# A mask added on POOL and a bias added by ScalarE in place of two VectorE operations, in the recurrence of a hybrid decoder layer

## Chip, cores and metric

The kernel runs on one core of a Trainium2 chip. The metric is the device time of one execution in microseconds (us), as the median of several runs. The profile shows one execution.

## What is computed

One decoder layer over 1024 prompt tokens and 8 sample tokens, with width 1024. A norm with modulation and the input projection come first, then three groups in parallel (RG-LRU, mLSTM, multi-scale pool), an output projection, and an MLP with squared ReLU. The change lies in the mLSTM group, four heads of width 96, which is worked in eight chunks of 128 tokens, one after the other:

```python
bcum = jnp.cumsum(lfb, axis=-1)
D = bcum[..., :, None] - bcum[..., None, :] + ib[..., None, :]
D = jnp.where(mask, D, -jnp.inf)
g = bcum + m[..., None]
m_t = jnp.maximum(g, jnp.max(D, axis=-1))
inter = jnp.exp(g - m_t)
S = jnp.einsum('bhtd,bhsd->bhts', qb, kb) * jnp.exp(D - m_t[..., None])
num = jnp.einsum('bhts,bhsd->bhtd', S, vb) + inter[..., None] * jnp.einsum('bhvk,bhtk->bhtv', C, qb)
...
C_new = decay[..., None, None] * C + jnp.einsum('bhs,bhsv,bhsk->bhvk', w, vb, kb)
```

The exponent `D - m_t` of a pair (t, s) is the sum of a term of t alone (the negated running maximum, once bcum is taken out of it), a term of s alone (ib - bcum), and the mask.

## The kernel before

Every engine has its own stream of instructions, written out by hand, with semaphores between them. `MIX_ORDER` is a table of steps that all engines walk through in the same order, each issuing what it has to do in a step; so a step's place in the table is its place in every queue. `D:u:c` is a dense product of the input projection, unit u (128 output features) and third c of the tokens (344 columns), three float32r matmuls per block because each factor is split into a high and a low part. The high parts are copies on ScalarE (`W_hi`, `Y_hi`), the low parts are differences on POOL (`W_lo`, `Y_lo`); steps `W:u`, `D:14:c` and later, `YD:c` and `POOLY` carry such splits. `ADA`, `ADT` and `ADM` work on the modulation, and `R:n` are loads of weights that ScalarE's queue issues. Between the dense products stand the small steps of the recurrence, with c now the chunk from 0 to 7:

- `LD:c`: SP loads keys, queries, values and `NM`, the negated running maxima of the chunk's tokens (128 columns of t for four heads, the same on all 128 partitions). `NM` has one buffer. The load of chunk c waits until `NM` has been read for chunk c - 1 (L884).
- `EX:c`: the exponent. On VectorE, `EX` = `NM` + the column of s, broadcast along t (L1885), then the minimum of that and the mask (L1886), both 128x512; then ScalarE takes the exponential in place (L1368). For c > 0 VectorE first waits for the product of chunk c - 1 that read `EX` (bank A).
- `S:c`: TensorE transposes the keys (L2498) and multiplies keys and queries (L2502). `SX:c`: VectorE weights the keys (L1892) and multiplies scores and exponential (L1895).
- `AB:c`: TensorE multiplies queries and state (L2514) and, once L1895 is done, scores and values (L2520). `NU`, `HN`, `HM` on VectorE build the normalised output (L1900 to L1919), with a square root on ScalarE between them (L1371); `U` and `CN` bring the state forward (L2528, L1923, L1925).
- `Y:c`, `YD:c`: the chunk's output is transposed (L2536), gated (L1936) and split.

ScalarE runs copies, exponential, square root, sigmoid and gelu (L1331). Some of these need another table of functions: then an ACT_TABLE_LOAD stands before the operation, at the same line. `SMB`, `SMC` are the sample tokens' branch on VectorE, `POOLV` to `POOLY` the pool group, whose matmuls (L2549) take the banks that `NU` frees.

```python
c = s[1]
if c == 0:
    tell(V.memset(CN[:], 0.0), cn_ready, 1)
    dve.wait_ge(ld_dec, 16)
    dve.wait_ge(ld_mask, 16)
else:
    wait_full(dve, ("A", c - 1))
dve.wait_ge(ld_nm, 16 * (c + 1))
link(V.tensor_tensor(EX[:], NM[:], wide(colh(0, c), LC), ALU.add))
tell(V.tensor_tensor(EX[:], EX[:], over(MASK[:], HEADS), ALU.min), ex_ready, c + 1)
```

Of the kernel before, what the change touches and what calls it, by code (L numbers as in the profile page):

```python
# [87 lines left out]
def unit_of(kind, t):  # L88
# [57 lines left out]
D:9:0  # L146
D:9:1 R:46 R:45 LD:1 ADM:16 EX:0 ADA:17:0 S:0 SX:0 ADA:17:1 W:11 AB:0 R:47
D:9:2 ADT:17 U:0 NU:0 HN:0 CN:0 ADM:17 HM:0 EX:1 ADA:18:0 SMK S:1 SX:1 SMB:0
D:10:0 LD:2
D:10:1 LD:3 AB:1 NU:1 ADA:18:1 U:1 CN:1 HN:1  # L150
D:10:2 HM:1 R:49 R:48 LD:4 EX:2 W:12
D:11:0 SMB:1 S:2 SX:2 AB:2 NU:2 ADT:18 U:2 CN:2 ADM:18 HN:2 R:50
D:11:1 SMB:2 HM:2 R:52 EX:3 ADA:19:0 S:3 SX:3
D:11:2 SMB:3 AB:3 ADA:19:1 W:13 LDO:0 R:51 NU:3
D:12:0 ADT:19 U:3 HN:3 HM:3 R:53 CN:3 ADM:19 LD:5 ADA:20:0 EX:4 R:55
D:12:1 S:4 SX:4 ADA:20:1 Y:0 R:54 SMC AB:4 NU:4
D:12:2 R:56 U:4 ADT:20 HN:4 W:14 YD:0 R:58 HM:4 LD:6
# [132 lines left out]
def build(nc, I, O):  # L290
# [24 lines left out]
    with ExitStack() as ctx:  # L315
# [482 lines left out]
        def _(sp):  # L798
# [26 lines left out]
            for s in plan:  # L825
# [41 lines left out]
                elif k == "LD":  # L867
# [210 lines left out]
        def _(pool):  # L1078
# [25 lines left out]
            for s in plan:  # L1104
# [108 lines left out]
        def _(act):  # L1213
# [55 lines left out]
            for s in plan:  # L1269
# [407 lines left out]
        def _(dve):  # L1677
# [78 lines left out]
            for s in plan:  # L1756
# [1129 lines left out]
```

## Time and profile before

| | |
|---|---|
| median of 3 runs | 1175.29 us (1174.09 to 1179.2) |
| the profiled execution's own time | 1175.78 us |
| its span | 1174.0 us |
| its mean granted TensorE clock | 0.982 of full speed |
| busy: PE, VectorE (DVE), ScalarE (ACT), POOL | 1124.6, 792.8, 473.4, 346.9 us |
| the eight chunks of the recurrence | from about 225 to 385 us |

The span is the time between the first and the last instruction of the execution that the profiler took. Busy time of an engine is the sum of its instructions; "idle before" names the time an engine stood still before an instruction and what released it. PE is TensorE, and "granted clock" is the share of 2.4 GHz at which it was allowed to run: 0.50 is 1.2 GHz.

### The profile page before, as it was taken

To read this page: it belongs to the slowest core of one execution; us is meant where nothing else is said; L and a number is where in the kernel's file an instruction comes from. 1 tells how busy PE (TensorE), PEld (TensorE's weight loads), DVE (VectorE), ACT (ScalarE), POOL (GpSimd) and SP (SyncE) were. 2 spreads that over 40 slices of the span, in tenths; PEclk is the share of its full clock that TensorE was granted. 3 is DMA by queue.
4 is the path that set the end of the run, shared out by engine and by line. 5 is a ranking of instruction groups with operands and counts; after the bars stand their busy time and mean duration, and the time that the engine had idled before them with its cause. 6 is when DMAs were issued, how large, how long until landed. Compare 5 with 4: busy or idle time off the path is not lost.

```text
span 1174.0 us, 19681 instructions
## 1 busy us (share of the span) xinstructions
PE 1124.6 (96%) x7237; PEld 1077.3 (92%) x7237; DVE 792.8 (68%) x1319; ACT 473.4 (40%) x780; POOL 346.9 (30%) x275
## 2 busy tenths in 40 slices
PE   4799999999989999999999999999999999999997
PEld 1598888888979999899999999999999999999996
DVE  4561455478775434678578878778778788788546
ACT  5551355655456344642233332332432433433431
POOL 0442011201434357764032022132131231231352
PEclk9699999998989999999999999999999999999998
DMA  8912523566523722111111111202102202111104
GB/s 302 326 57 88 142 90 126 177 180 218 176 87 113 269 90 73 54 55 37 37 36 55 54 37 55 71 18 71 56 16 75 68 18 72 53 50 58 37 1 145
DMA packets 67846, 109.85 MB, mean 94 GB/s; under 512 B 6435, under 2 KB 42567, under 8 KB 67399
## 3 DMA queue, kind: packets, MB, share of 16 engines
q1 hardware_dynamic: 57574, 84.88, 22.0%
q10 hardware_dynamic: 10208, 24.12, 6.6%
q8 instruction: 41, 0.67, 0.2%
q14 instruction: 23, 0.18, 0.0%
HBM read 96.81 MB, written 12.18 MB: 93 GB/s over the span
## 4 chain that ended last, share of the span: by engine, by line
PE 82%; DVE 9%; ACT 3%; DMA 2%; issue 1%; POOL 1%; SPq 1%; ACTq 0%; POOLq 0%; DVEq 0%
PE D L2407 7%; PE D L2409 7%; PE D L2408 7%; PE D L2591 6%; PE D L2593 5%; PE D L2592 5%; PE X L2593 5%; PE X L2591 5%; PE X L2592 5%; PE X L2663 5%; PE X L2664 5%; PE X L2665 5%; PE D L2663 2%; PE D L2665 2%; PE D L2664 2%; DMA RAWW<-in_WADA 2%
## 5 line engine op out<-in xcount | busy, mean ns | idle before, releaser
L2407 PE MATMUL D<-H_hi,W_hi 128*128 128x344 f32 x472 | 158.6, 336 | 3.7 <-POOL H_lo L1087 3.1
L2409 PE MATMUL D<-H_hi,W_lo 128*128 128x344 f32 x472 | 152.4, 323 | 0.0
L2408 PE MATMUL D<-H_lo,W_hi 128*128 128x344 f32 x472 | 152.4, 323 | 0.0
L1087 POOL TENSOR_TENSOR Y_lo<-FU,Y_hi 128x344 fp32r<-128x344 f32 (+3 forms) x84 | 100.1, 1194 | 154.2 <-ACT Y_hi L1521 88.5
L1082 POOL TENSOR_TENSOR W_lo<-RAWW,W_hi 128x1024 fp32r<-128x1024 f32 x25 | 61.6, 2465 | 182.5 <-ACT W_hi L1234 182.2
L1087 POOL TENSOR_TENSOR Y_lo<-EY,Y_hi 128x344 fp32r<-128x344 f32 (+1 forms) x24 | 38.3, 1598 | 216.3 <-ACT Y_hi L1521 144.5
L2407 PEld LDWEIGHTS D<-H_hi,W_hi 128*128 128x128 f32 x472 | 90.5, 192 | 11.8 <-issue 7.6
L2408 PEld LDWEIGHTS D<-H_lo,W_hi 128*128 128x128 f32 x472 | 90.3, 191 | 0.9 <-issue 0.5
L2409 PEld LDWEIGHTS D<-H_hi,W_lo 128*128 128x128 f32 x472 | 90.2, 191 | 0.0
L2215 DVE SCALAR_TENSOR_TENSOR X<-X,MOD 128x344 f32<-128x344 f32 (+1 forms) x138 | 75.7, 566 | 9.2 <-PE X L2665 9.0
L2663 PE MATMUL X<-Y_hi,W_hi 128*128 128x344 f32 x252 | 80.7, 320 | 0.0
L2664 PE MATMUL X<-Y_lo,W_hi 128*128 128x344 f32 x252 | 80.6, 320 | 0.0
L2665 PE MATMUL X<-Y_hi,W_lo 128*128 128x344 f32 x252 | 80.5, 319 | 0.0
L2017 DVE SCALAR_TENSOR_TENSOR X<-D,MOD,X 128x344 f32<-128x344 f32 (+1 forms) x72 | 41.3, 573 | 45.4 <-PE D L2593 24.7
L2407 PE MATMUL D<-Y_hi,W_hi 128*128 128x344 f32 x192 | 62.0, 323 | 1.5 <-POOL W_lo L1082 1.5
L1099 POOL TENSOR_TENSOR SS<-SS,SQ 128x344 f32<-128x344 f32 x45 | 43.3, 963 | 65.9 <-ACT SQ L1430 40.5
L1087 POOL TENSOR_TENSOR Y_lo<-KEPT,Y_hi 128x344 fp32r<-128x344 f32 x24 | 26.4, 1098 | 120.7 <-ACT Y_hi L1521 120.7
L2408 PE MATMUL D<-Y_lo,W_hi 128*128 128x344 f32 x192 | 61.3, 319 | 0.0
L2409 PE MATMUL D<-Y_hi,W_lo 128*128 128x344 f32 x192 | 61.3, 319 | 0.0
L1556 ACT ACTIVATE W_hi<-RAWW 128x1024 fp32r<-128x1024 f32 x30 | 31.8, 1059 | 64.3 <-PE X L2665 55.6
L2378 PE MATMUL X<-RAWW,CTX 128*32 128x256 f32 x384 | 35.7, 461 | 19.5 <-DMA RAWW<-in_WADA 19.4
L1087 POOL TENSOR_TENSOR H_lo<-FU,H_hi 128x344 fp32r<-128x344 f32 (+2 forms) x33 | 29.9, 914 | 66.2 <-ACT FU L1252 50.7
(416 smaller groups left out, 3455.1 us busy)
## 6 DMA issues: line engine op xcount, KB each, us to landing
RAWW<-in_W SPq DMA_DIRECT2D x76, 512.0 KB, 3.6
RAWW<-in_WADA ACTq DMA_DIRECT2D x28, 512.0 KB, 4.1
RAWW<-in_WADA SPq DMA_DIRECT2D x20, 512.0 KB, 8.0
RAWW<-in_W ACTq DMA_DIRECT2D x18, 512.0 KB, 3.7
X0T<-in_x SPq DMA_DIRECT2D x3, 1376.0 KB, 12.8
out_y<-OUTN SPq DMA_DIRECT2D x24, 172.0 KB
X<-in_x SPq DMA_DIRECT2D x8, 344.0 KB, 5.3
NM<-nm_d SPq DMA_DIRECT2D x8, 256.0 KB, 5.3
```

What stands on the lines that cost most here:

```text
L1082: nc.gpsimd.tensor_tensor(lo_v, RAWW[:, raw, :] if src is None else src[:], hi_v.bitcast(F32), ALU.subtract).then_inc(w_lo_ready, 1)
L1087: nc.gpsimd.tensor_tensor(lo_v, fu_v, hi_v.bitcast(F32), ALU.subtract).then_inc(lo_ready, 1)
L2215: V.scalar_tensor_tensor(out=X[:, m, c * CH:c * CH + w], in0=ps[:, 0:w], scalar=MOD[:, 5 * KT + m, 0:1], in1=X[:, m, c * CH:c * CH + w], o ...
L2407: T.matmul(out, w_h, hi[:, kt, a:b], start=(kt == 0), stop=False)
L2408: T.matmul(out, w_h, lo[:, kt, a:b], start=False, stop=False)
L2409: one = T.matmul(out, w_l, hi[:, kt, a:b], start=False, stop=(kt == KT - 1))
L2591: T.matmul(out, w_h, hi(kt), start=(kt == 0 and not onto), stop=False, skip_group_check=onto)
L2592: T.matmul(out, w_h, lo(kt), start=False, stop=False, skip_group_check=onto)
L2593: one = T.matmul(out, w_l, hi(kt), start=False, stop=(kt == n - 1), skip_group_check=onto)
L2663: T.matmul(bank[:, 0:CH], w_hi[:, a:a + P], h, start=(start and k == 0), stop=False, skip_group_check=onto)
L2664: T.matmul(bank[:, 0:CH], w_hi[:, a:a + P], l, start=False, stop=False, skip_group_check=onto)
L2665: one = T.matmul(bank[:, 0:CH], w_lo[:, a:a + P], h, start=False, stop=(stop and k == 1), skip_group_check=onto)
```

## The change

POOL gets a step of its own, `NX:c`, which adds the mask to `NM` in place once its load has landed. ScalarE's `EX:c` reads `NM` and writes `EX`, one head at a time, with the column of s as the bias of the exponential. The two VectorE operations are gone, and the waits that stood before them are now ScalarE's (for bank A of chunk c - 1, and for POOL's add). SP's load of the next `NM` waits for the exponential in place of the VectorE operation. The mask is 0 or -3e38, so that adding it and taking the minimum give the same exponential.

```diff
-D:9:1 R:46 R:45 LD:1 ADM:16 EX:0 ADA:17:0 S:0 SX:0 ADA:17:1 W:11 AB:0 R:47
-D:9:2 ADT:17 U:0 NU:0 HN:0 CN:0 ADM:17 HM:0 EX:1 ADA:18:0 SMK S:1 SX:1 SMB:0
+D:9:1 R:46 R:45 LD:1 ADM:16 NX:0 EX:0 ADA:17:0 S:0 SX:0 ADA:17:1 W:11 AB:0 R:47
+D:9:2 ADT:17 U:0 NU:0 NX:1 HN:0 CN:0 ADM:17 HM:0 EX:1 ADA:18:0 SMK S:1 SX:1 SMB:0
...
-D:14:0 Y:2 ADM:21 EX:6 YD:2
+D:14:0 Y:2 ADM:21 NX:6 EX:6 YD:2
...
-D:15:0 U:6 Y:4 POOL:1:0 R:62 CN:6 POOLY:1:0 ADA:23:0 EX:7 POOL:1:1 W:16 R:64 YD:4
+D:15:0 U:6 Y:4 POOL:1:0 R:62 CN:6 POOLY:1:0 ADA:23:0 NX:7 EX:7 POOL:1:1 W:16 R:64 YD:4
...
                     if c >= 1:
-                        sp.wait_ge(ex_ready, c)
+                        sp.wait_ge(ex_exp, c)
...
+                elif k == "NX":
+                    if s[1] == 0:
+                        pool.wait_ge(ld_mask, 16)
+                    pool.wait_ge(ld_nm, 16 * (s[1] + 1))
+                    nc.gpsimd.tensor_tensor(NM[:], NM[:], over(MASK[:], HEADS), ALU.add).then_inc(nm_masked, 1)
...
                 elif k == "EX":
-                    act.wait_ge(ex_ready, s[1] + 1)
-                    nc.scalar.activation(EX[:], EX[:], ACT.Exp).then_inc(ex_exp, 1)
+                    c = s[1]
+                    if c == 0:
+                        b, n = use[("G4",)]
+                        act.wait_ge(x_free[b], n + 1)
+                    else:
+                        wait_full(act, ("A", c - 1))
+                    act.wait_ge(nm_masked, c + 1)
+                    for h in range(HEADS):
+                        one = nc.scalar.activation(EX[:, h, :], NM[:, h, :], ACT.Exp, bias=colh(0, c)[:, h:h + 1])
+                    one.then_inc(ex_exp, 1)
...
                 elif k == "EX":
-                    c = s[1]
-                    if c == 0:
+                    if s[1] == 0:
                         tell(V.memset(CN[:], 0.0), cn_ready, 1)
                         dve.wait_ge(ld_dec, 16)
-                        dve.wait_ge(ld_mask, 16)
-                    else:
-                        wait_full(dve, ("A", c - 1))
-                    dve.wait_ge(ld_nm, 16 * (c + 1))
-                    link(V.tensor_tensor(EX[:], NM[:], wide(colh(0, c), LC), ALU.add))
-                    tell(V.tensor_tensor(EX[:], EX[:], over(MASK[:], HEADS), ALU.min), ex_ready, c + 1)
```

`NX:2` to `NX:5` stand likewise ahead of their `EX`, further away from it: behind `NU:1`, `NU:2`, `NU:3` and `NU:4`.

POOL's queue through the stretch of the recurrence, before and after as one piece of the difference. L1082 splits weights, L1128 is the new add.

```order
-L1082 TENSOR_TENSOR W_lo<-RAWW,W_hi 128x1024 x12
+L1082 TENSOR_TENSOR W_lo<-RAWW,W_hi 128x1024 x8
+L1128 TENSOR_TENSOR NM<-NM,MASK 128x512
+L1082 TENSOR_TENSOR W_lo<-RAWW,W_hi 128x1024
+L1128 TENSOR_TENSOR NM<-NM,MASK 128x512 x2
+L1082 TENSOR_TENSOR W_lo<-RAWW,W_hi 128x1024
+L1128 TENSOR_TENSOR NM<-NM,MASK 128x512
+L1082 TENSOR_TENSOR W_lo<-RAWW,W_hi 128x1024
+L1128 TENSOR_TENSOR NM<-NM,MASK 128x512 x2
+L1082 TENSOR_TENSOR W_lo<-RAWW,W_hi 128x1024
 L1087 TENSOR_TENSOR Y_lo<-FU,Y_hi 128x3x128 x2
```

The adds of chunks 0 to 5 stand between the weight splits of the units 10 to 14. Further down the same queue, the adds of chunks 6 and 7 stand between the splits of the gated outputs (L1087).

```order
 L1087 TENSOR_TENSOR Y_lo<-FU,Y_hi 128x344
+L1128 TENSOR_TENSOR NM<-NM,MASK 128x512
 L1087 TENSOR_TENSOR Y_lo<-FU,Y_hi 128x3x128
 L1087 TENSOR_TENSOR Y_lo<-FU,Y_hi 128x344 x2
 L1087 TENSOR_TENSOR Y_lo<-FU,Y_hi 128x3x128
 L1087 TENSOR_TENSOR Y_lo<-FU,Y_hi 128x344 x5
+L1128 TENSOR_TENSOR NM<-NM,MASK 128x512
 L1082 TENSOR_TENSOR W_lo<-RAWW,W_hi 128x1024
```

The first of them now follows the split of `D:14:0`, the second the two splits of `D:15:0` and `POOLY:1:0`.

ScalarE's queue around `EX:6`, with what each instruction waits for, before:

```order
L1331 ACTIVATE GT<-D 128x344 [waits dense0_full]
L1239 ACTIVATE Y_hi<-FU 128x344 [waits full_ready]
L1368 ACT_TABLE_LOAD
L1368 ACTIVATE EX<-EX 128x512 [waits ex_ready]
L1239 ACTIVATE Y_hi<-FU 128x3x128 [waits full_ready]
L1331 ACT_TABLE_LOAD [waits full_ready]
L1331 ACTIVATE GT<-D 128x344 [waits dense1_full]
```

and after:

```order
L1336 ACTIVATE GT<-D 128x344 [waits dense0_full]
L1244 ACTIVATE Y_hi<-FU 128x344 [waits full_ready]
L1380 ACT_TABLE_LOAD [waits nm_masked]
L1380 ACTIVATE EX<-NM,COL 128x128 [waits X1_full]
L1380 ACTIVATE EX<-NM,COL 128x128 x3
L1244 ACTIVATE Y_hi<-FU 128x3x128 [waits full_ready]
L1336 ACT_TABLE_LOAD [waits full_ready]
L1336 ACTIVATE GT<-D 128x344 [waits dense1_full]
```

The one exponential has become four, and the wait for the add (`nm_masked`) stands at the table load, where the load had no wait before; this holds for all eight chunks.

## Rows read from the trace of the kernel before

**Rows 1.** The page, busy time and share of the span of the matmul engine.

```profile
...
PE 1124.6 (96%) x7237; PEld 1077.3 (92%) x7237; DVE 792.8 (68%) x1319; ACT 473.4 (40%) x780; POOL 346.9 (30%) x275
...
```

**Rows 2.** Waits of PE, 225 to 385 us: engine line <- released by: us, times, longest.

```profile
...
PE X L2549 <- DVE NUM L1903: 3.7, 1, 3.7
PE X L2520 <- DVE EX L1895: 2.9, 3, 1.7
PE D L2407 <- POOL W_lo L1082: 1.5, 1, 1.5
...
```

**Rows 3.** Windows: us, busy (x) of PE, PEld, DVE, ACT, POOL; PEclk, DMA share, GB/s.

```profile
...
232.00:240.00 8.00, 7.00 (x60) 5.85 (x60) 5.12 (x12) 2.64 (x4) 0.00 (x0) 1.00 0.91 274
...
268.00:275.00 7.00, 7.00 (x34) 7.00 (x35) 4.69 (x13) 1.39 (x2) 0.65 (x1) 0.54 0.52 174
...
382.00:392.00 10.00, 8.48 (x54) 8.36 (x54) 4.86 (x5) 3.44 (x6) 5.48 (x5) 1.00 0.64 211
...
```

**Rows 4.** The page, DMA issues: x count, KB each, us to landing.

```profile
...
NM<-nm_d SPq DMA_DIRECT2D x8, 256.0 KB, 5.3
```

**Rows 5.** Groups by line and form, ScalarE: xcount | busy us, mean ns | idle before.

```profile
...
L1368 ACT ACTIVATE EX<-EX 128x512 f32<-128x512 f32 x8 | 5.1, 632 | 5.8 <-DVE EX L1886 5.7
...
```

**Rows 6.** The same view for POOL.

```profile
...
L1060 POOL TENSOR_TENSOR PA<-ST 128x1023 f32<-128x1023 f32 x1 | 1.9, 1890 | 0.0
...
L1209 POOL TENSOR_TENSOR OUTN<-XG,INVS 128x344 f32<-128x344 f32 x2 | 1.8, 908 | 6.2 <-ACT INVS L1673 6.2
...
```

**Rows 7.** One line of the program, L1362: duration ns min/median/max, first and last start.

```profile
...
L1362 ACT ACTIVATE GR<-GR,MPC x1: 405/405/405, 134.4 to 134.4; 36x128 f32<-36x128 f32 x1
...
```

**Rows 8.** Timelines at chunk 0: start us, us, engine line op xcount [idle before <- releaser].

```profile
...
233.29 0.69 DVE L1885 TENSOR_TENSOR EX<-NM,COL 128x512 f32<-128x512 f32 x1 [1.25 <-DMA NM<-nm_d]
...
233.96 1.28 ACT L1368 ACT_TABLE_LOAD   x1 [1.35 <-issue]
...
235.97 0.69 DVE L1895 TENSOR_TENSOR EX<-X,EX 128x512 f32<-128x512 f32 x1 [0.67 <-ACT EX L1368]
...
236.72 1.13 PE L2520 MATMUL X<-VB,EX 128*128 128x97 f32 x8 [1.00 <-DVE EX L1895]
...
```

**Rows 9.** Timelines at chunk 2.

```profile
...
264.65 0.63 ACT L1368 ACTIVATE EX<-EX 128x512 f32<-128x512 f32 x1
...
267.08 0.69 DVE L1895 TENSOR_TENSOR EX<-X,EX 128x512 f32<-128x512 f32 x1
...
267.82 1.41 PE L2520 MATMUL X<-VB,EX 128*128 128x97 f32 x8 [1.67 <-DVE EX L1895]
...
```

**Rows 10.** Timelines of POOL and DVE where both read SBUF, 286 us.

```profile
...
286.67 2.40 POOL L1082 TENSOR_TENSOR W_lo<-RAWW,W_hi 128x1024 fp32r<-128x1024 f32 x1 [18.02 <-ACT W_hi L1234]
...
286.86 2.62 DVE L1912 TENSOR_TENSOR HM<-NUM,SM 128x384 f32<-128x384 f32 x1
...
```

**Rows 11.** Timelines at chunk 6.

```profile
...
327.99 1.12 POOL L1087 TENSOR_TENSOR Y_lo<-FU,Y_hi 128x344 fp32r<-128x344 f32 x1 [2.28 <-ACT Y_hi L1239]
...
330.85 0.52 ACT L1239 ACTIVATE Y_hi<-FU 128x384 fp32r<-128x384 f32 x1 [0.53 <-DVE FU L1936]
...
332.69 0.46 ACT L1331 ACTIVATE GT<-D 128x344 f32<-128x344 f32 x1
...
334.32 0.69 DVE L1895 TENSOR_TENSOR EX<-X,EX 128x512 f32<-128x512 f32 x1
...
335.07 1.13 PE L2520 MATMUL X<-VB,EX 128*128 128x97 f32 x8 [0.19 <-DVE EX L1895]
...
```

**Rows 12.** Timelines at chunk 7.

```profile
...
355.41 2.27 POOL L1087 TENSOR_TENSOR Y_lo<-FU,Y_hi 128x344 fp32r<-128x344 f32 x2 [3.34 <-ACT Y_hi L1239]
...
358.27 0.64 ACT L1368 ACTIVATE EX<-EX 128x512 f32<-128x512 f32 x1 [0.51 <-DVE EX L1886]
...
358.81 1.04 ACT L1234 ACTIVATE W_hi<-RAWW 128x1024 fp32r<-128x1024 f32 x1
...
366.82 0.46 ACT L1331 ACTIVATE GT<-D 128x344 f32<-128x344 f32 x1 [1.05 <-PE D L2409]
...
```

More of the change, by code:

```diff
@@ L146 @@
 D:9:0
-D:9:1 R:46 R:45 LD:1 ADM:16 EX:0 ADA:17:0 S:0 SX:0 ADA:17:1 W:11 AB:0 R:47
-D:9:2 ADT:17 U:0 NU:0 HN:0 CN:0 ADM:17 HM:0 EX:1 ADA:18:0 SMK S:1 SX:1 SMB:0
+D:9:1 R:46 R:45 LD:1 ADM:16 NX:0 EX:0 ADA:17:0 S:0 SX:0 ADA:17:1 W:11 AB:0 R:47
+D:9:2 ADT:17 U:0 NU:0 NX:1 HN:0 CN:0 ADM:17 HM:0 EX:1 ADA:18:0 SMK S:1 SX:1 SMB:0
 D:10:0 LD:2
-D:10:1 LD:3 AB:1 NU:1 ADA:18:1 U:1 CN:1 HN:1
+D:10:1 LD:3 AB:1 NU:1 NX:2 ADA:18:1 U:1 CN:1 HN:1
 D:10:2 HM:1 R:49 R:48 LD:4 EX:2 W:12
-D:11:0 SMB:1 S:2 SX:2 AB:2 NU:2 ADT:18 U:2 CN:2 ADM:18 HN:2 R:50
+D:11:0 SMB:1 S:2 SX:2 AB:2 NU:2 NX:3 ADT:18 U:2 CN:2 ADM:18 HN:2 R:50
 D:11:1 SMB:2 HM:2 R:52 EX:3 ADA:19:0 S:3 SX:3
-D:11:2 SMB:3 AB:3 ADA:19:1 W:13 LDO:0 R:51 NU:3
+D:11:2 SMB:3 AB:3 ADA:19:1 W:13 LDO:0 R:51 NU:3 NX:4
 D:12:0 ADT:19 U:3 HN:3 HM:3 R:53 CN:3 ADM:19 LD:5 ADA:20:0 EX:4 R:55
-D:12:1 S:4 SX:4 ADA:20:1 Y:0 R:54 SMC AB:4 NU:4
+D:12:1 S:4 SX:4 ADA:20:1 Y:0 R:54 SMC AB:4 NU:4 NX:5
 D:12:2 R:56 U:4 ADT:20 HN:4 W:14 YD:0 R:58 HM:4 LD:6
@@ L512, in build @@
         ld_nm, ld_o, ld_mask = sem("ld_nm"), sem("ld_o"), sem("ld_mask")
-        ex_ready, ex_exp, cn_ready = sem("ex_ready"), sem("ex_exp"), sem("cn_ready")
+        nm_masked, ex_exp, cn_ready = sem("nm_masked"), sem("ex_exp"), sem("cn_ready")
         z_ready, z_root, hm_ready = sem("z_ready"), sem("z_root"), sem("hm_ready")
```

## The prediction, made before the changed kernel was run

> **What bounds the kernel now.** I read the page first: TensorE is busy 96% of the span, VectorE 68%, ScalarE 40%, POOL 30% [rows 1]. So work taken off VectorE is worth only what TensorE waits for VectorE, and that is the second view. All eight chunks of the recurrence run between 225 and 385 us, and nothing outside that stretch is touched. There TensorE's waits are few: 3.7 us in one piece before the pool group's matmuls, 2.9 us in three pieces for the exponent times scores (L1895), 1.5 us for a weight split (L2407) [rows 2]. The last two numbers matter most: only the 2.9 us sit directly behind the operations that the change moves. Third, the granted clock by stretch. From 232 to 240 us, a wait of 1.00 us included, it was 1.00; from 268 to 275 us, right behind a wait of 1.67 us, it was 0.54, nearly all of it at 1.2 GHz; from 382 to 392 us, a wait of 1.5 us included, it was 1.00 again [rows 3, 8, 9]. The stretch at 0.54 lost 7.0 x 0.46 = 3.2 us of work, more than the wait ahead of it. So a wait just above those that were harmless costs its own length and may cost 3.2 us more; whether it does is not in my hands.
>
> **What is removed.** VectorE loses 16 operations of 0.69 us [rows 8], 11 us in all. Where its queue is what TensorE waits for, this is a gain of up to 1.4 us per chunk. It is that only at chunk 2, below. At chunks 1, 3, 4 and 5 TensorE does not wait for the product of scores and exponent: the cover is the dense products of the next unit, matmuls that need nothing of the recurrence. If that cover were gone, each would be worth its 1.4 us.
>
> **What is added, with prices.** (a) POOL adds 128x512, never seen here. Two-input float operations on POOL took 0.908 us for 344 columns and 1.890 us for 1023 [rows 6]; between them a column costs 1.45 ns, so 512 come to 1.15 us. These two rows are also the bounds, 0.9 and 1.9; I take 1.15, since 512 lies between them and near the first. (b) ScalarE runs four exponentials of 128 columns with a column as bias where it ran one of 512 in 0.632 us [rows 5]. The one exponential of 128 columns with a bias column took 0.405 us [rows 7], and a following ScalarE operation starts 0.10 us before its forerunner ends (358.27 + 0.64 against 358.81) [rows 12]. Four cost 3 x 0.305 + 0.405 = 1.32 us. Bounds: 0.63 if the column is free, 1.62 with no overlap. (c) The wait for POOL now hangs on the load of the exponential's table, as the order of ScalarE shows; before, the load had no wait and ran while VectorE still worked (233.96 to 235.24, while the second VectorE operation ended at 233.29 + 2 x 0.69 = 234.7) [rows 8]. So its 1.28 us follow POOL's add where they lay beside VectorE's. (d) The next load of the row maxima waits for the exponential, 1 to 4 us later than for VectorE's add. It lands 5.3 us after issue [rows 4], and the starts of two chunks' products lie 13 us apart or more; I cost that at nothing from chunk 1 on, and the stores and loads of o behind it on SP's queue likewise. If a load came late after all, POOL's add would wait for it and ScalarE with it.
>
> POOL's queue is in order, so an add that waits for its load holds what is behind it: splits of weights, which TensorE needs only a unit later. The other direction costs: chunks 6 and 7 have their add placed behind splits which wait for ScalarE.
>
> **The sum, chunk by chunk.**
> Chunk 0. The row maxima land at 233.25, VectorE starts at 233.29 and multiplies at 235.97; TensorE waits 1.00 us for it [rows 8]. Now: POOL 233.3 to 234.45, table to 235.8, exponentials to 237.15, product at 237.25. Later by 1.3 us: +1.3. TensorE's wait becomes 2.3 us.
> Chunk 2. All runs 1.3 us later. VectorE is 1.4 us freer and the exponentials, begun at 264.65 + 1.3, end at 267.27; the product starts at 267.35 where 267.08 + 1.3 = 268.38 would stand [rows 9]. Gain 1.0 us, and the wait of 1.67 us shrinks to 0.7 us. ScalarE, not VectorE, is then late next. -1.0.
> Chunk 6. POOL's add follows the split that ends at 329.11; added and signalled at 330.35, table at 331.65, exponentials at 332.95. The copy of Y_hi behind them began at 330.85 and now begins at 332.85, so the gelu at 332.69, the product at 334.32 and TensorE's matmuls at 335.07 all come 2.0 us later [rows 11]. VectorE's windows of the pool group follow them, and the wait of 3.7 us behind is not a cushion, because VectorE is what it waits for [rows 2]. +2.0.
> Chunk 7. The add follows two splits that end at 357.68: 358.9, table 360.2, exponentials 361.5 instead of 358.91. The gelu at 366.82 had 1.05 us of idle before it, which takes part of the 2.6 us [rows 12]. From there a closed chain runs to the split for L2407 and its 1.5 us [rows 2]. +1.5.
> Together +1.3 - 1.0 + 2.0 + 1.5 = +3.8 us. The clock: a wait of 0.7 us should spare the low stretch at 268, -3.2; of the two waits that grow well past 1.67 us (2.3 at chunk 0, about 3.0 at the end) I expect one to bring a low stretch, +3.2. The profiled execution took 1175.78 us with a span of 1174.0 and stands 0.5 us above the median of 1175.29. So 1175.78 + 3.8 = 1179.6, or **1179.1** as a median: 0.3% slower, inside what a measurement here can tell from no change (0.5%, 5.9 us).
>
> POOL's price, row against page: the rows give 1.15 us, 1.7 times VectorE's 0.69. The Trainium skill, "GPSIMD Engine Reference", section "Engine selection", advises VectorE for elementwise work and puts two-input operations on GpSimd at about twice its time. That would be 1.38 us and add 0.2 us at each of three chunks, 0.7 us in all: 1179.8.
>
> **The rivals.**
> *Both grown waits lower the clock.* 3.8 - 3.2 + 6.4 = +7.0: 1182.3. For it: 2.3 and 3.0 us are both longer than the 1.67 us behind which the clock fell. Against: part of the loss at chunk 0 fits into a later wait. It decides from the point where chunk 0's product starts more than about 0.7 us late. This one ends slower.
> *POOL holds up VectorE.* A VectorE operation on two SBUF tiles took 2.62 us, ending as POOL's split of 2.40 us did, where a wider one takes 0.69 [rows 8, 10]. The eight adds are 9.2 us of such time on POOL. Most meet VectorE idle or reading PSUM. Chunk 5's would land on the samples' chain near 297 us, behind which TensorE already waits, and cost up to 1.2 us, chunk 2's half of that: +3.8 + 1.8 = +5.6, 1180.9, and with one more low stretch 1184.1. The Trainium skill says the same in the same reference, section "Key points": GpSimd shares its SBUF interfaces with VectorE, contending with instructions of two SBUF inputs. The trace agrees by its 2.62 us.
> *No low stretch at all.* +3.8 - 3.2 = +0.6: 1175.9. For it: no wait up to 1.5 us was followed by one. Against: 2.3 and 3.0 us are longer.
> *VectorE was the bound after all.* Then 16 x 0.72 with gaps, 11.5 us, come back: 1163.8. Against: TensorE is at 96%, and its waits for the product are 2.9 us in all [rows 1, 2].
> That the change does not do what it says would show as an unchanged VectorE; the order shows its two operations gone, so I give it nothing.
>
> **How the numbers follow.** Forecast 0.50, its own bounds 1176 to 1182 (prices of POOL and bias at their ends); both waits lower the clock 0.22; POOL holds up VectorE 0.15; no low stretch 0.10; VectorE the bound 0.03. Slower by over 5.9 us (above 1181.2): all of the first rival, 0.12 of the second, 0.03 of the forecast's upper end, 0.37. Faster by as much: 0.03. Between: 0.60. The range from 1175.5 to 1185.0 leaves out a tenth at either end.
>
> **What would show it.** Right: VectorE busy 11 us less, ScalarE 5 us more, POOL 9 us more; the table load at L1380 starting after POOL's add at chunks 0, 6 and 7; the product of chunk 0 at 237.2; the wait at 268 below 1 us and the clock at 1.00 behind it; the exponentials of chunks 6 and 7 about 2 us later than before, relative to the matmuls beside them. Wrong: the table load starting before the add ends; TensorE's wait at chunk 0 unchanged; or a total wait between 225 and 385 us that falls by more than 2 us.

## The result and the profile after

| | before | after |
|---|---|---|
| median | 1175.68 us (12 runs) | 1180.96 us (12 runs, 1178.87 to 1186.17) |
| profiled execution, its span | 1175.78, 1174.0 us | 1181.11, 1179.3 us |

The ratio is 1.0052, with a 95% interval of 1.0039 to 1.0065, or 6.1 us of 1175. The quotient of the two medians is a little less, 1.0045: they lie 5.3 us apart, as do the profiled executions. The sum had 3.8 us. The interval lies clear of 1, so the sign is certain; the size is known to a microsecond or two.

The page of the kernel after, busy times by engine:

```profile
PE 1126.4 (96%) x7237; PEld 1078.5 (91%) x7237; DVE 782.9 (66%) x1303; ACT 478.5 (41%) x804; POOL 356.7 (30%) x283
```

Against [rows 1], VectorE has 16 instructions and 9.9 us less, ScalarE 24 instructions and 5.1 us more, POOL 8 instructions and 9.8 us more. The forecast had 11 us less, 5 more and 9 more. So the work moved as the change says, and the time rose. What TensorE waited for between 225 and 390 us tells more (line, what released it: us in total, times, longest):

```profile
PE X L2526 <- DVE EX L1901: 6.0, 3, 2.8
PE X L2555 <- DVE NUM L1909: 2.4, 1, 2.4
PE X L2542 <- DVE MOD L1730: 2.0, 1, 2.0
...
PE X L2542 <- DVEq L1947: 1.3, 1, 1.3
...
```

L2526 and L1901 are L2520 and L1895 of before: 2.9 us of waits for the product of scores and exponential [rows 2] became 6.0. The wait before the pool group, L2555, fell from 3.7 to 2.4 us: part of what chunk 6 lost was taken out of it.

To keep effects apart I cut out the stretch in which the change acts: from the first selector matmul of chunk 0 (PE, L2392 before, L2398 after) to the start of the weight split at the end of chunk 7 (POOL, L1082). The windows of before and of after (length; busy PE, PEld, DVE, ACT, POOL; granted clock; DMA share, GB/s):

```profile
223.87:381.13 157.26, 147.40 (x1043) 136.04 (x1044) 116.05 (x234) 82.86 (x121) 45.91 (x36) 0.96 0.53 161
```

```profile
223.67:385.46 161.79, 148.27 (x1043) 136.18 (x1044) 105.53 (x217) 87.90 (x145) 55.87 (x44) 0.96 0.52 158
```

The stretch is 4.5 us longer. TensorE is idle 161.79 - 148.27 = 13.5 us of it, 9.9 before: 3.7 us are waiting, 0.9 us matmuls that take longer. From the end of the stretch to the end of the span it is 792.9 us before and 793.8 after (1174.0 - 381.13 and 1179.3 - 385.46), and 792.4 to 794.1 in the runs below, whose code there is the same, so I make nothing of that 1.0 us. Ahead of the stretch one execution differs from the next by more: the first selector matmul starts anywhere from 221.5 to 224.9 us, in kernels that are the same up to there. That is why times are compared by the ratios of many runs, and mechanisms within the stretch.

The granted clock after, in windows of PE alone (length, busy, clock, DMA share, GB/s), and one of before near the same place of the program as the last:

```profile
238.00:242.00 4.00, 3.67 (x16) 0.57 1.04 283
268.00:275.00 7.00, 5.87 (x47) 1.00 0.86 288
337.00:341.00 4.00, 4.00 (x23) 0.57 0.35 129
347.00:355.00 8.00, 7.90 (x26) 0.57 0.71 196
```

```profile
342.00:351.00 9.00, 6.24 (x18) 4.85 (x19) 8.08 (x16) 6.30 (x11) 4.28 (x4) 0.62 0.43 120
```

The low stretch at 268 us [rows 3] is gone, as forecast. Two new ones of half its size stand at 238 and 337 us (4.00 x 0.43 = 1.7 us lost each). The one behind the pool group's wait was there before too (9.00 x 0.38 = 3.4 us) and still is (8.00 x 0.43 = 3.4). In all, the clock lost 6.8 us before and 6.8 us after.

**Chunk 0 after**, timeline:

```profile
233.58 1.27 POOL L1128 TENSOR_TENSOR NM<-NM,MASK 128x512 f32<-128x512 f32 x1 [7.22 <-DMA NM<-nm_d]
234.92 1.28 ACT L1380 ACT_TABLE_LOAD   x1 [2.52 <-POOL NM L1128]
236.22 1.28 ACT L1380 ACTIVATE EX<-NM,COL 128x128 f32<-128x128 f32 x4
237.58 0.69 DVE L1901 TENSOR_TENSOR EX<-X,EX 128x512 f32<-128x512 f32 x1 [3.93 <-ACT EX L1380]
238.33 2.02 PE L2526 MATMUL X<-VB,EX 128*128 128x97 f32 x8 [2.82 <-DVE EX L1901]
```

Three operations in a row, none beside another: ScalarE stood idle 2.52 us and then loaded a table. In [rows 8] that load ran while VectorE was still at the second of its two operations.

**Chunk 2 after:**

```profile
267.86 1.28 ACT L1380 ACTIVATE EX<-NM,COL 128x128 f32<-128x128 f32 x4
269.23 0.69 DVE L1901 TENSOR_TENSOR EX<-X,EX 128x512 f32<-128x512 f32 x1 [0.48 <-ACT EX L1380]
269.97 1.13 PE L2526 MATMUL X<-VB,EX 128*128 128x97 f32 x8 [1.13 <-DVE EX L1901]
```

The wait is 1.13 us where [rows 9] had 1.67, and VectorE now waits for ScalarE (0.48 us).

**POOL and VectorE between chunks 3 and 4:**

```profile
285.68 2.40 POOL L1082 TENSOR_TENSOR W_lo<-RAWW,W_hi 128x1024 fp32r<-128x1024 f32 x1 [11.58 <-ACT W_hi L1239]
286.52 1.57 DVE L1913 SCALAR_TENSOR_TENSOR SM<-NUM 128x4 f32<-128x4 f32 x1
288.03 1.27 POOL L1128 TENSOR_TENSOR NM<-NM,MASK 128x512 f32<-128x512 f32 x1
288.12 1.20 DVE L1914 TENSOR_TENSOR SM<-SM,COL 128x4 f32<-128x4 f32 x1
```

Two VectorE operations on four columns end with the POOL operation they run beside, one with the split (288.08), the next with the new add (289.30). Before, both took 0.17 us, and one wider operation lost 2.06 us to the split (2.62 us where it takes 0.56 elsewhere) [rows 10]. So POOL holds up VectorE in both kernels.

**Chunk 6 after:**

```profile
328.03 0.92 POOL L1087 TENSOR_TENSOR Y_lo<-FU,Y_hi 128x344 fp32r<-128x344 f32 x1 [2.25 <-ACT Y_hi L1244]
328.91 1.29 POOL L1128 TENSOR_TENSOR NM<-NM,MASK 128x512 f32<-128x512 f32 x1
330.28 1.28 ACT L1380 ACT_TABLE_LOAD   x1 [2.32 <-POOL NM L1128]
331.57 1.28 ACT L1380 ACTIVATE EX<-NM,COL 128x128 f32<-128x128 f32 x4
...
334.58 0.46 ACT L1336 ACTIVATE GT<-D 128x344 f32<-128x344 f32 x1
...
336.96 1.76 PE L2526 MATMUL X<-VB,EX 128*128 128x97 f32 x8 [2.04 <-DVE EX L1901]
```

Split, add, table load, exponentials, each released by the one before. The gelu moved from 332.69 [rows 11] to 334.58 and TensorE's wait from 0.19 to 2.04 us.

**Chunk 7 after:**

```profile
358.13 1.97 POOL L1087 TENSOR_TENSOR Y_lo<-FU,Y_hi 128x344 fp32r<-128x344 f32 x2 [3.92 <-ACT Y_hi L1244]
360.06 1.29 POOL L1128 TENSOR_TENSOR NM<-NM,MASK 128x512 f32<-128x512 f32 x1
361.43 1.28 ACT L1380 ACT_TABLE_LOAD   x1 [2.33 <-POOL NM L1128]
362.72 0.40 ACT L1380 ACTIVATE EX<-NM,COL 128x128 f32<-128x128 f32 x1
...
370.97 0.46 ACT L1336 ACTIVATE GT<-D 128x344 f32<-128x344 f32 x1
```

The same chain. The gelu of [rows 12], 366.82 before, starts at 370.97 and has no idle time left before it.

Where the 4.5 us came from can be read at TensorE's waits, each counted from the first selector matmul (before 223.87, after 223.67). The two marks of before that no row above shows:

```profile
304.19 0.58 PE L2392 MATMUL X<-SEL,ADS 128*128 128x9 f32 x4 [0.90 <-DVEq L1941]
...
344.76 2.63 PE L2549 MATMUL X<-ST,BDP 128*128 128x344 f32 x4 [3.72 <-DVE NUM L1903]
```

and of after:

```profile
303.69 0.58 PE L2398 MATMUL X<-SEL,ADS 128*128 128x9 f32 x4 [0.90 <-DVEq L1947]
...
346.90 2.03 PE L2555 MATMUL X<-ST,BDP 128*128 128x344 f32 x4 [2.44 <-DVE NUM L1909]
```

| mark | before | after | late by | since the mark above | of it idle | of it busy |
|---|---|---|---|---|---|---|
| scores times values, chunk 0 | 12.85 | 14.66 | 1.8 | +1.8 | +1.8 | 0 |
| the same, chunk 2 | 43.95 | 46.30 | 2.35 | +0.5 | -1.0 | +1.55 |
| selector, behind chunk 4 | 80.32 | 80.02 | -0.3 | -2.65 | +0.3 | -2.95 |
| scores times values, chunk 6 | 111.20 | 113.29 | 2.1 | +2.4 | +2.4 | 0 |
| pool group's matmuls | 120.89 | 123.23 | 2.3 | +0.25 | -1.3 | +1.55 |
| weight split, end of chunk 7 | 157.26 | 161.79 | 4.5 | +2.2 | +1.45 | +0.75 |

The last two columns part each piece into the time that TensorE stood still and the time that its matmuls took, from the windows between the marks. The matmuls are the same ones, so the busy column is the clock: a new low stretch behind chunk 0, the one at 268 us gone, a new one at 337 us. The 0.75 us of the last line is the old stretch at the pool group. Before, its first 1.9 us (342.9 to 344.76) lay in TensorE's wait and cost nothing; after, nearly all of it lies behind the wait.

### The profile page after: what moved, and what is told of

The parts are those of the page before. It is cut to its first block, busy times and chain, and to the rows that moved or that the text cites. A ratio compares the mean times of both kernels' runs of the same rounds, so it can differ in the third digit from the quotient of the medians.

```text
span 1179.3 us, 19696 instructions
## 1 busy us (share of the span) xinstructions
PE 1126.4 (96%) x7237; PEld 1078.5 (91%) x7237; DVE 782.9 (66%) x1303; ACT 478.5 (41%) x804; POOL 356.7 (30%) x283
## 4 chain that ended last, share of the span: by engine, by line
PE 79%; DVE 9%; ACT 5%; DMA 2%; POOL 2%; issue 2%; SPq 1%; ACTq 0%; POOLq 0%; DVEq 0%
PE D L2413 6%; PE D L2415 6%; PE D L2414 6%; PE D L2597 5%; PE D L2599 5%; PE D L2598 5%; PE X L2599 5%; PE X L2597 5%; PE X L2598 5%; PE X L2669 5%; PE X L2671 5%; PE X L2670 5%; PE D L2669 2%; PE D L2671 2%; PE D L2670 2%
## 5 line engine op out<-in xcount | busy, mean ns | idle before, releaser
L1087 POOL TENSOR_TENSOR Y_lo<-FU,Y_hi 128x344 fp32r<-128x344 f32 (+3 forms) x84 | 99.5, 1187 | 154.6 <-ACT Y_hi L1534 87.4
L1082 POOL TENSOR_TENSOR W_lo<-RAWW,W_hi 128x1024 fp32r<-128x1024 f32 x25 | 61.7, 2468 | 147.1 <-ACT W_hi L1239 146.8
L1087 POOL TENSOR_TENSOR Y_lo<-EY,Y_hi 128x344 fp32r<-128x344 f32 (+1 forms) x24 | 38.4, 1599 | 216.3 <-ACT Y_hi L1534 144.5
L1087 POOL TENSOR_TENSOR Y_lo<-KEPT,Y_hi 128x344 fp32r<-128x344 f32 x24 | 26.3, 1098 | 121.8 <-ACT Y_hi L1534 121.8
L1087 POOL TENSOR_TENSOR H_lo<-FU,H_hi 128x344 fp32r<-128x344 f32 (+2 forms) x33 | 29.9, 914 | 66.1 <-ACT FU L1257 50.5
## 6 DMA issues: line engine op xcount, KB each, us to landing
X0T<-in_x SPq DMA_DIRECT2D x3, 1376.0 KB, 12.5
```

The lines of the kernel that those rows point to most:

```text
L1082: nc.gpsimd.tensor_tensor(lo_v, RAWW[:, raw, :] if src is None else src[:], hi_v.bitcast(F32), ALU.subtract).then_inc(w_lo_ready, 1)
L1087: nc.gpsimd.tensor_tensor(lo_v, fu_v, hi_v.bitcast(F32), ALU.subtract).then_inc(lo_ready, 1)
```

## The experiments

My theory: the loss is the table load and four exponentials in series behind an add, and POOL's queue where the add stands behind splits. The rivals: POOL's adds as such, by holding up VectorE; and the clock. Each kernel below was timed in five rounds beside the kernel before. Stretch and TensorE's idle time in it are cut as above; the clock column is the time that the granted clock lost in it, (1 - clock) times length.

| kernel | median | ratio to before, interval | stretch | idle | clock |
|---|---|---|---|---|---|
| before | 1175.0 | | 157.3 | 9.9 | 6.8 |
| after | 1181.0 | 1.0052 (1.0039 to 1.0065) | 161.8 | 13.5 | 6.8 |
| waits swapped | 1176.85 | 1.0013 (1.0 to 1.0026) | 156.9 | 10.7 | 5.1 |
| adds of 6, 7 ahead | 1178.17 | 1.0037 (1.0022 to 1.0053) | 157.8 | 11.5 | 5.1 |
| both | 1176.37 | 1.0007 (0.9994 to 1.002) | 157.6 | 11.3 | 5.1 |
| chunk 0 as before | 1177.78 | 1.0031 (1.0015 to 1.0046) | 159.1 | 11.1 | 6.8 |
| only chunk 0 changed | 1179.47 | 1.0037 (1.0025 to 1.0049) | 161.9 | 12.0 | 10.2 |
| no POOL | 1180.31 | 1.0041 (1.0025 to 1.0058) | 163.5 | 12.5 | 10.2 |
| no POOL, swapped | 1175.22 | 1.0003 (0.9986 to 1.0021) | 159.4 | 10.2 | 8.5 |
| no bias | 1177.92 | 1.0032 (1.0017 to 1.0048) | 159.9 | 12.0 | 6.8 |
| no bias, adds ahead | 1175.24 | 1.001 (0.9989 to 1.003) | 155.0 | 10.2 | 3.4 |
| chunks 1 to 5 changed | 1173.85 | 0.9995 (0.9978 to 1.0012) | 155.9 | 9.6 | 5.1 |
| the same, swapped | 1173.64 | 1.0004 (0.9987 to 1.0021) | 155.7 | 10.9 | 3.4 |
| chunk 0 as before, both | 1174.98 | 0.9997 (0.9984 to 1.0011) | 156.9 | 10.3 | 5.1 |

Stretch, idle and clock are of one execution each, the ratios of all runs; where they differ the ratio decides. Two ratios whose intervals overlap are not surely different. The median of before is that of the last runs, 1174.98 to 1175.68 us in the others; each ratio is to the runs of before beside it.

### ScalarE's two waits swapped

```diff
 c = s[1]
+act.wait_ge(nm_masked, c + 1)
 if c == 0:
     b, n = use[("G4",)]
     act.wait_ge(x_free[b], n + 1)
 else:
     wait_full(act, ("A", c - 1))
-act.wait_ge(nm_masked, c + 1)
 for h in range(HEADS):
```

The last wait written goes to the table load, the one before it to the first exponential. Nothing else differs.

> Only ScalarE's two waits before the exponentials change places, so that the table load carries the wait for bank A (long fulfilled) and the first exponential carries the wait for POOL's add. Mine (the table load behind the wait is part of the loss at chunks 0, 6 and 7): the product of chunk 0 starts 1.3 us earlier than in the changed kernel, TensorE's wait there falls from 2.8 to about 1.5 us, gelu of chunks 6 and 7 come 1.3 us earlier each; 3 x 1.3 = 3.8 us, and 3.2 us more if the low stretch of the clock at 238 us goes: 1174 to 1177 us. Rival (POOL's adds hold up VectorE, or the four exponentials cost it): the load's place does nothing, 1181 us.

Measured: 1.0013, 4.6 us less than with the change (0.0039 x 1175), and the two intervals do not meet; of idle time 2.8 us less. TensorE's wait at chunk 0 fell from 2.82 to 1.59 us, with a low stretch behind it as before. The timeline at chunk 0, and at chunk 6:

```profile
232.05 1.27 POOL L1128 TENSOR_TENSOR NM<-NM,MASK 128x512 f32<-128x512 f32 x1 [6.63 <-DMA NM<-nm_d]
232.74 1.28 ACT L1380 ACT_TABLE_LOAD   x1 [1.29 <-DVE KW L1898]
234.04 1.28 ACT L1380 ACTIVATE EX<-NM,COL 128x128 f32<-128x128 f32 x4
...
326.54 1.29 POOL L1128 TENSOR_TENSOR NM<-NM,MASK 128x512 f32<-128x512 f32 x1
...
327.86 1.28 ACT L1380 ACTIVATE EX<-NM,COL 128x128 f32<-128x128 f32 x4 [0.98 <-POOL NM L1128]
```

The load now runs ahead of POOL's add at chunk 6, under the split (it started at 325.60) and half under it at chunk 0, where it waited for the bank. Order alone gives back most of the loss: shown.

### The adds of chunks 6 and 7 ahead of POOL's splits

```diff
-D:13:2 ADT:21 R:59 U:5 CN:5
-D:14:0 Y:2 ADM:21 NX:6 EX:6 YD:2
+D:13:2 ADT:21 R:59 U:5 NX:6 CN:5
+D:14:0 Y:2 ADM:21 EX:6 YD:2
...
-    HM:6
-D:15:0 ... ADA:23:0 NX:7 EX:7 ...
+    NX:7 HM:6
+D:15:0 ... ADA:23:0 EX:7 ...
```

> Only the places of POOL's adds of chunks 6 and 7 in its queue change: each is put ahead of the splits it followed. Mine: the exponentials of chunk 6 end about 2.0 us and those of chunk 7 about 2.6 us earlier, which is worth 2.0 + 1.5 = 3.5 us: 1177.5 us, with chunk 0 as in the changed kernel. Rival (POOL holds up VectorE wherever it works): the adds cost the same at another place, 1181 us. If the row maxima land late, POOL stands still for them and the splits come late: slower than 1181 us.

Measured: 1.0037, 1.8 us less by the ratios, 2.8 by the medians; the intervals overlap, so by the times alone this gain is not shown. The trace shows where it comes from. POOL's add stands at 325.76, the table load at 328.34 waits for nothing, and TensorE has no wait left for chunk 6's product, where it was 2.04 us. In exchange the add meets work of VectorE: it took 1.66 us instead of 1.29, and TensorE's wait for `MOD` right behind it is 2.36 us where it was 2.00.

### Both

> The two waits of ScalarE swapped, and the adds of chunks 6 and 7 placed ahead of the weight splits. My theory: the table load behind the add is the larger loss (the swap alone gave 4.3 us back), and the place of the adds has little left to give once the load runs under them: chunk 6's wait of 0.71 us goes, and about 1 us at chunk 7; the split for the dense product at the end of that stretch (379.59 with the swap alone) comes near 378.3, TensorE's wait for the recurrence's product at chunk 6 is gone, and the median is about 1175.3 us. Rival A, the two gains add up: 1174.1 or less. Rival B, POOL's adds in the earlier place meet VectorE's pairs of SBUF tiles and give it back: 1176.9 or more.

Measured: 1.0007, between my 1175.3 and rival B, and not to be told from the swap alone (0.0006 apart, with intervals of 0.0013 either way). Rival A, that the gains add up (1174.1, a ratio of 0.9992), lies just outside the interval. Both edits take the table load from behind the add at chunks 6 and 7, so they compete for the same microseconds.

### Chunk 0 alone, both ways

The first kernel gives chunk 0 its two VectorE operations and single exponential back (`OLD = (0,)`), the second does so for all others (`OLD = (1, ..., 7)`). In both, SP's load of the next row maxima waits for the exponential.

```diff
+elif k == "EX" and s[1] in OLD:
+    act.wait_ge(ex_ready, n_old(s[1]))
+    nc.scalar.activation(EX[:], EX[:], ACT.Exp).then_inc(ex_exp, 1)
```

> Chunk 0 as before the change (VectorE adds and takes the minimum, one exponential), chunks 1 to 7 as changed. Mine: TensorE's wait at chunk 0 is 1.0 us again and no low stretch follows; the wait at chunk 2 stays under 1 us and the clock at 1.00 there too; the delays at chunks 6 and 7 remain: 1175.7 - 1.0 - 3.2 + 3.5 = 1175.0 us. Rival (the loss is spread over all chunks, by POOL beside VectorE or by ScalarE's 5 us more): a seventh or an eighth of 5.3 us is saved, 1180.3 us.

> Chunk 0 as changed, chunks 1 to 7 as before (but SP's load of the next row maxima still waits for the exponential). Mine: a wait of 2.8 us at chunk 0 with a low stretch behind it, +1.6 + 3.2 us less what later waits take in; whether the wait at chunk 2 (1.67 us) still brings its own low stretch decides between 1180 and 1177 us. Rival (spread loss): an eighth of 5.3 us, 1176.4 us.

Measured: 1.0031 without the change at chunk 0, where I had 1175.0 us and 1177.78 were measured: a miss. With it there alone, 1.0037, as expected. Taken by themselves the parts cost 3.6 and 4.3 us, together more than the 6.1 us of the whole (0.0052 x 1175), though by no more than the intervals allow. The traces show one reason why they need not add up. With chunk 0 alone changed, lateness of 1.6 us reaches chunk 2, whose VectorE is no freer than before, and the wait there grows to 2.15 us; with three full low stretches the clock lost 10.2 us in all. With all chunks changed, chunk 2 gives 1.0 us back and spares its low stretch. With chunk 0 as before, TensorE waited 0.93 us for the product, but two short waits for transfers came together, and the clock was low from 243 to 248 us, a low stretch that I had not expected (a second one, from 325 to 330 us, stood behind the wait of 2.00 us for `MOD`):

```profile
242.43 0.64 PE L2402 MATMUL X<-RAWW,CTX 128*32 128x256 f32 x8 [0.70 <-DMA RAWW<-in_WADA]
...
243.68 0.78 PE L2522 MATMUL X<-IDN,K 96*128 96x96 f32 x4 [0.61 <-DMA VB<-v_d]
```

### POOL left out; and with the waits swapped

VectorE adds the mask to the row maxima in place, ScalarE the column. The second kernel swaps ScalarE's waits as above.

```diff
...
-nc.gpsimd.tensor_tensor(NM[:], NM[:], over(MASK[:], HEADS), ALU.add).then_inc(nm_masked, 1)
...
+tell(V.tensor_tensor(NM[:], NM[:], over(MASK[:], HEADS), ALU.add), nm_masked, s[1] + 1)
```

> POOL is left out: VectorE adds the mask in place (0.69 us), ScalarE adds the column as bias in four exponentials, the table load keeps its place behind the add. My theory (the load behind the add, and the four exponentials, are the price; POOL's share is its 0.6 us longer add and its queue at chunks 6 and 7): chunk 0's load starts at 234.0, the exponentials end at 236.6, its product starts at 236.7 (237.58 with the change, 235.97 before), the exponentials of chunks 6 and 7 need not wait for POOL's splits, VectorE is busy about 788 us, and the median is 1177 to 1178. Rival, contention of POOL with VectorE is what cost most: without POOL it is as fast as before or faster, 1175 or less.

> The kernel in which VectorE adds the mask in place, ScalarE the column, and POOL does nothing, now with ScalarE's two waits swapped, so that the table load no longer waits for VectorE's add. Stretch and idle are taken from the first selector matmul of chunk 0 to the start of the weight split at the end of chunk 7: before 157.3 us with 9.9 us of TensorE idle, with the change 161.8 and 13.5, without POOL and unswapped 163.5 and 12.5. My theory, the table load behind the add is the larger loss: every exponential whose add comes late ends 1.2 us earlier, the wait at chunk 0 falls from 2.2 to about 0.9 us and that at chunk 2 from 1.8 to about 0.6 us, both without a low stretch behind them; the stretch is about 158.5 us and the median 1176. Rival, the four exponentials and VectorE's add in its queue are the cost: it stays above 161 us, and the median at 1179 or more.

Measured: 1.0041 without POOL, 1180.31 us; I had 1177 to 1178. Leaving POOL's adds out saves nothing that the ratios can show (1.0041 against 1.0052, with overlapping intervals) and 1.0 us of idle time, though VectorE takes eight adds back for it. So the adds as such, and their contention, are not the main cost: this rival falls, but for a share of about 1 us. The miss is the clock again. VectorE multiplied for chunk 0 at 235.79, and waits of 2.16 us there and 1.78 us at chunk 2 both brought a full low stretch. Swapped, the ratio is 1.0003, 4.5 us less, the same amount as with POOL, and again the intervals do not meet. The table load without POOL, then swapped:

```profile
232.37 0.69 DVE L1890 TENSOR_TENSOR NM<-NM,MASK 128x512 f32<-128x512 f32 x1 [1.66 <-DMA NM<-nm_d]
233.13 1.28 ACT L1375 ACT_TABLE_LOAD   x1 [1.86 <-DVE NM L1890]
```

```profile
231.41 0.69 DVE L1890 TENSOR_TENSOR NM<-NM,MASK 128x512 f32<-128x512 f32 x1 [1.79 <-DMA NM<-nm_d]
231.47 1.28 ACT L1375 ACT_TABLE_LOAD   x1 [1.28 <-issue]
232.77 1.28 ACT L1375 ACTIVATE EX<-NM,COL 128x128 f32<-128x128 f32 x4
```

The waits I had expected to fall to 0.9 and 0.6 us fell to 1.58 and 1.19. At chunk 0 the chain is then no longer than before: from the first operation on the row maxima to the multiplication it is 2.72 us (231.41 to 234.13), in the kernel before 2.68 (233.29 to 235.97), with the change 4.00. The wait is longer than the 1.00 us of before because the load landed 0.5 us later. So the second VectorE operation that is gone pays for the three more exponentials, once the table load is out of the way.

### The bias left out; and with the adds ahead

POOL adds the mask, VectorE the column into `EX`, ScalarE takes one exponential of 512 columns, its table load without a wait. The second kernel puts the adds of chunks 6 and 7 ahead of the splits.

```diff
...
+dve.wait_ge(nm_masked, s[1] + 1)
+tell(V.tensor_tensor(EX[:], NM[:], wide(colh(0, s[1]), LC), ALU.add), ex_ready, s[1] + 1)
```

> POOL adds the mask (1.28 us), VectorE adds the column (0.69 us), ScalarE takes one exponential of 512 columns, whose table load has no wait ahead of it. My theory: chunk 0's product starts near 236.0 as before and the wait there is about 1.1 us; chunks 6 and 7 still have their add behind POOL's splits, 1.5 to 2 us later than before; median 1176.5 us, within 1.5 us of the kernel before. Rival, POOL's adds themselves (contention on SBUF and its queue) are the cost: 1179 or more, near the change's 1181.

> POOL adds the mask, VectorE the column, ScalarE takes one exponential; the adds of chunks 6 and 7 now ahead of POOL's weight splits. My theory: what this way cost over the kernel before (idle 12.0 us against 9.9 in the stretch) is POOL's queue at chunks 6 and 7; chunk 6's wait of 1.5 us goes, chunk 7's exponential is on time, idle is about 10.5 us, one low stretch fewer, and the median is 1175.5. Rival, VectorE held up by the add that waits for POOL (2.18 us for one of them) is the cost: 1177.5 or more, as with the adds behind the splits.

Measured: 1.0032, then 1.001. Here no table load stands behind POOL, and 3.8 us are lost all the same, more than I had (1176.5 us, 1177.92 measured): the wait at chunk 0 was 2.01 us for an expected 1.1. With the adds ahead 1.2 us are left. At chunk 6 TensorE's wait was 1.52 us with the add behind the split and gone with it ahead. So POOL's queue is a second place where time is lost, beside the table load. Its size is less sure: 2.6 us by the ratios, whose intervals overlap, and the traces differ by 3.4 us of clock, half of it at chunk 0, ahead of anything that this edit moves.

### Chunks 1 to 5 changed; the same with the waits swapped

> Chunks 0, 6 and 7 as before the change, chunks 1 to 5 as changed, nothing swapped. My theory: chunks 1 to 5 are where the change costs nothing and spares the wait of 1.7 us at chunk 2, so TensorE's idle time in the stretch is 9 to 9.5 us (9.9 before), chunk 6 starts no later against the matmuls beside it, and the median is 1174 to 1175.5, as before or a little less. Rival, POOL's adds beside VectorE's pairs (the small operations of 1.57 and 1.20 us near 287 us) cost as much as the freed VectorE gives: idle of 10.5 us or more and a median of 1176.5 or more.

> As the kernel with only chunks 1 to 5 changed, with ScalarE's two waits swapped. My theory: in these chunks POOL adds the mask long before the column is there, so the wait that the table load carries is that for the column, at every one of them; the swap lets the load run before it and each exponential starts 1.2 us earlier, but TensorE waits for none of them except at chunk 2. So 0 to 0.8 us less than without the swap: median 1173.8 to 1175. Rival: the exponentials 1.2 us earlier meet other work of VectorE and move a wait elsewhere, 1175.5 or more.

Measured: 0.9995 and 1.0004, both no different from before. Where the add has room in POOL's queue, the change costs nothing and what it frees is worth nothing that can be measured; the idle time went from 9.9 to 9.6 us in the one and to 10.9 in the other, where 1.0 us of it is a longer wait at the selector behind chunk 4 (1.86 us for 0.90). On the swap my expectation had the waits the wrong way round: here it puts the wait for the bank on the table load. It made no difference, since neither wait held the load in chunks 2 to 5.

### Chunk 0 as before, waits swapped, adds ahead

> Chunk 0 as before the change (two VectorE operations, one exponential), chunks 1 to 7 as changed with the waits swapped and the adds of chunks 6 and 7 ahead of the splits. My theory: chunk 0's wait is 0.9 us and no low stretch stands behind it; what the changed way gives at chunk 2 stays (no wait of 1.67 us and no low stretch at 268 us), so this is the fastest of all, about 1173.5 us, that is 1.7 us faster than the kernel before. Rival: a low stretch comes somewhere else instead, as behind the waits near 243 us when chunk 0 alone went back: then 1176, no better than the kernel before.

Measured: 0.9997. I had expected 1.7 us less than before. The idle time is 10.3 us. The load of chunk 0's row maxima landed 1.2 us later after the first selector matmul than in the trace of before, TensorE waited 1.67 us there, and the clock fell. So no kernel that was run is faster than the one before by more than the measurement's uncertainty.

## Why the prediction was right

The forecast was a loss of 3.8 us from four places, and a clock that gives back as much as it takes. The trace shows all four places with their mechanisms, close to their size, and 4.5 us in the stretch: 3.7 of waiting and 0.9 of slower matmuls.

- **Chunk 0, +1.3.** Measured 1.8 at the mark. POOL's add started 9.91 us after the selector matmul where VectorE's started 9.42 us after it, so 0.5 us is a later landing, and 1.3 us the chain. VectorE multiplied at 237.58; 237.25 had been forecast.
- **Chunk 2, -1.0.** Measured -1.0. VectorE's last reduction of chunk 1 came 3.4 us late, counted from the selector matmul (260.01 before, 263.17 after), the product of chunk 2 only 2.35. The wait is 1.13 us rather than 0.7, and not below the 1 us that I had named as a sign, because the clock had made everything ahead of it late too.
- **Chunk 6, +2.0.** Measured +2.4, of which 0.5 us is the longer wait for `MOD` at 328 us (2.00, before 1.46), and 1.9 us the exponentials. That longer wait stands in every kernel in which chunk 5 has its four exponentials, without POOL's adds too (2.0 to 2.4 us), and is not in the sum.
- **Chunk 7, +1.5.** Measured +1.45 of idle time. The exponentials ended 5.3 us late against the selector matmul (358.91, then 364.00), the gelu 4.35: the 1.05 us of idle time took its part, as forecast. Of the 5.3, 2.9 were there before the splits (the gelu of the dense product ahead, 353.75, then 356.46), so the add and what hangs on it made 2.4 us for a forecast 2.6.
- **Between chunk 2 and the selector behind chunk 4, nothing in the sum.** Measured +0.3 of idle time, a wait of 0.31 us for `MOD` at 294 us; the wait at the selector is 0.90 us in both. That is all that the second rival, POOL beside VectorE, can have cost here; I had up to 1.8 us for it. Without POOL's adds and with the waits swapped the idle time of this piece is as long, 1.2 us.
- **The clock, -3.2 and +3.2.** By the granted clock -3.4 and +1.7 +1.7, equal sums, but not as I argued. Both grown waits lowered the clock, as the first rival says, and each for half of what I priced; that the two halves made up the one stretch forecast was luck. In matmul time it was -2.95, +1.55 and +1.55, and +0.75 for the stretch at the pool group, which no row of mine had: +0.9 for a forecast 0. The stretch at 337 us cost little, because TensorE would otherwise have waited longer for VectorE before the pool group (-1.3 us of idle time). I had written that this wait was no cushion. It is none for ScalarE's lateness and it is one for slow matmuls.
- **Prices.** POOL's add, the tile's view after:

```profile
L1380 ACT ACTIVATE EX<-NM,COL x32: 384/387/403, 236.2 to 363.6; 128x128 f32<-128x128 f32 x32
...
L1128 POOL TENSOR_TENSOR NM<-NM,MASK x8: 1267/1288/1554, 233.6 to 360.1; 128x512 f32<-128x512 f32 x8
```

It took 1.29 us, where two rows of other widths gave 1.15 and bounds of 0.9 and 1.9. The four exponentials took 1.28 us, forecast 1.32. The Trainium skill's rule of about twice VectorE's time ("GPSIMD Engine Reference", "Engine selection") gave an estimate of 1.38; against VectorE's 0.69 us the trace gives 1.87 times, nearer to the rule than to my rows.

Against the sum, the stretch was off by +0.5 at chunk 0, +0.4 at chunk 6, +0.3 in the middle chunks, -1.3 at the pool group and +0.9 by the clock: +0.8, as 4.5 stands to 3.8 within rounding. Up to 1.0 us more lies behind the stretch, where nothing was changed. The size was right in part because misses of opposite sign met. The step that carried the verdict, (c), that the table load would stand behind the add, is what the swap of two lines tests, and it was worth 4.6 us with POOL and 4.5 without. That is more than I gave it: 1.28 us at each of chunks 0, 6 and 7 is 3.8, and part of chunks 6 and 7 was hidden. The clock lost 1.7 us less in the swapped kernel's trace, which is of the size of the surplus; that it is the cause is not shown.

## What to carry to other kernels

When an operation moves to an idle engine, follow the order of waits on the engine that reads it: a table load in front of an activation takes one of the waits written before it, and two swapped lines decided here whether 1.28 us ran beside the add or after it. Place an operation on the idle engine's queue before the work that is itself waiting for others, or its own lateness comes with it. And ask what the relieved engine is late for: VectorE lost 10 us of work and TensorE waited for its product longer (6.0 us for 2.9), because the chain to the products of chunks 0 and 6 had grown.

## What was not expected of the hardware

- **No length of a wait tells whether the clock falls.** TensorE's clock stayed at 2.4 GHz behind waits of 1.00, 1.13, 1.40, 1.46, 1.65, 2.00 and 2.36 us, and fell to 1.2 GHz behind waits of 1.23, 1.58, 1.67, 1.78 and again 2.00 us. It fell behind 3.7 us every time. Two kernels at chunk 0, first one with a wait of 1.65 us (bias left out, adds ahead), then one with a wait of 1.23 us (chunks 1 to 5 changed), PE's windows behind it:

```profile
235.00:240.00 5.00, 4.53 (x31) 1.00 1.00 293
```

```profile
235.00:239.00 4.00, 4.00 (x19) 0.59 1.07 322
```

  The low stretches lost 1.7 or 3.4 us each, and nothing between. Over the stretch they sum to between 3.4 and 10.2 us in the kernels above, a spread wider than any other term of this case. What decides whether the clock falls is left open.
- **The load of chunk 0's row maxima** reached its first reader 9.1 to 10.6 us after the first selector matmul, in kernels that do the same up to there. That alone can move the wait at chunk 0 by more than 1 us.
- **An operation on four columns** of VectorE took 1.57 and 1.20 us beside POOL, where it takes 0.17.
- **A table load costs its own 1.28 us and no more.** In the kernel before, an activation of another table ended at 244.79 us, the load began at 244.81 and the square root behind it at 246.10; after, the exponentials started 1.30 us after the load did (234.92 to 236.22). The Trainium skill ("ScalarE: Activation LUTs", "What ACT_TABLE_LOAD costs") gives 1.28 us for the load and about 1.38 us of drain on top for each switch. The trace agrees on the first; the second isn't there, and the measurement decides. The same section's figures for an activation with a column as bias give an estimate of 387 ns for 128 columns, and the trace has 387.
